# A decoder layer's up-projection: weight blocks and the T2 operand exchange their places in memory

## The chip, the cores and the metric

The kernel runs on 1 core of one Trainium2 chip. The metric is the device time of one execution in microseconds, the median of several runs. All arithmetic is in float32: each operand is split into a rounded high part and a rest (low part), and each product is three matmuls (low by high, high by low, high by high).

## The reference

One layer of a decoder trunk over 1024 tokens of width 1024: three token mixers, gated and merged, an output projection with a residual, then a convolutional feed-forward block. The change lies where the output projection ends and the up-projection begins.

```python
merged = gates[:, :, 0] * y_attn + gates[:, :, 1] * y_conv + gates[:, :, 2] * y_cross
h = h + merged @ w_out[l]

hn = rms_norm(h, ffn_norm_w[l])
up = causal_depthwise_conv(hn @ w_up[l], ffn_conv_w[l], ffn_conv_b[l])   # width 3
a, gt = jnp.split(up, 2, axis=-1)
h = h + (jax.nn.silu(gt) * a) @ w_down[l]
```

D_FF is 2816, so `hn @ w_up` has 22 pairs of 128 value columns and 128 gate columns.

## The kernel before

**Stages and engines.** The program is a list of stages. Each stage gives one function per engine (`sync`, `tensor`, `scalar`, `gpsimd`, `vector`), and every engine runs its own list in order. Engines meet at semaphores only; the order of the work is written out by hand. SyncE issues the loads. ScalarE rounds to high parts (`nc.scalar.copy` into a float32r tile), VectorE makes low parts (source less high part). SBUF addresses are given by hand with `at(name, offset, ...)`.

**Output projection (`w_out_stage`).** It has two halves of 512 columns (j = 0 and 1), each with 8 token tiles (t) of 128 tokens; a tile is 24 matmuls into one of two PSUM banks. Its weights come through a ring of 8 slots: `stage` (raw, the first 16 KiB of the memory used), `whi` (next 16 KiB) and `wlo` (next). The weights of the second half are split at j = 0, t = 7. VectorE evicts each tile with the residual added (line 2047). In the second half ScalarE stores each finished row tile to memory and squares it (lines 2011 and 326), GpSimd makes the row scale from pairs of tiles (lines 332 and 335), VectorE scales the pair (line 341, called from `scale`), and TensorE transposes it: batches 0 and 1 between the matmuls of tiles 4 and 5, batch 2 in tile 7 (line 1662), batch 3 in the next stage (`h_last_pe`, line 1685). The transposed pairs of tiles are the four buffers `xt`. Tiles 4 and 5 start with a wait for the row scaling of their batch.

**Up-projection (`up_stage`).** Each pair U of column blocks is one level of a Strassen-like scheme: seven products instead of eight, each of 12 matmuls (4 k-tiles by 3). The weight blocks 1, 2 and 4 are read from `u_raw`; 5, 6, 7 and 3 are sums and differences of blocks (`up_dve_sum`, lines 1821 to 1829, into `u_sums`). All seven are split into `u_hi` (ScalarE, line 1801) and `u_lo` (VectorE, line 1805). The moving operands are quarters of the normalised, transposed h (`act_hi`, `act_lo`) for products 1, 2 and 3 and the combinations T1 (product 5), T2 (6), T3 (7) and T4 (4). Each T has two halves q = 0, 1, and for each half a sum on VectorE (line 1747), a high part on ScalarE (line 1754) and a low part on VectorE (line 1759). `T_HALVES` gives the order of these splits, `T_SUMS` that of the sums. The T are made once, at the entry of the stage, and serve all pairs.

The accumulators of products 1, 6, 5 and 3 of a pair share one PSUM bank. After each of the first three ScalarE copies it out (s1, q1, q2: lines 1838, 1845, 1852), and the next product waits for that copy: 5 waits for `q1_done`, 3 waits for `q2_done`. In `pair_act`, the steady order of ScalarE, q1 is followed by the high parts 6 and 7 of the next pair and then by q2.

TensorE enters the stage with products 1 and 2 of pair 0. Then comes product 1 of pair 1 "ahead" (its blocks lie apart, in `u_next`), the transposes of batch 3, product 2 of pair 1 ahead, and products 6, 7, 5, 3, 4 of pair 0. From pair 1 on the order `middle` repeats: 6, 7, 5, the next pair's 1, 3, 4, the next pair's 2.

**Memory around the change.** T2 lies in the stage ring's raw slots, T3 in `whi`, T4 in `wlo`. The blocks lie in the region behind `h_rows` (`U_W`): two `u_raw` buffers, `u_hi`, `u_lo`, and then 8 KiB that `u_sums` and `u_next` share. The blocks and sums of pair 0 are made in the first half of the output projection (`first_pairs`, steps 2 to 7), the ahead parts of pair 1 at steps 8 and 9. The sums of pair 1 are made in `pair_dve` of pair 0 and wait until both ahead products are through.

**Down-projection.** Its first two pieces are split inside the last pair (`first_split`, `down_lows`); `d_stage`, `d_hi`, `d_lo` and `gs` lie in the low 28 KiB.

## Time and profile before

| | us |
|---|---|
| runs of the kernel before | 1985.51, 1983.98, 1985.40 |
| median | 1985.4 |
| profiled execution | 1986.32 |
| its span, first to last instruction | 1984.5 |

| engine | busy share of the span |
|---|---|
| TensorE matmul (PE) | 98% |
| TensorE weight load (PEld) | 83% |
| VectorE (DVE) | 55% |
| ScalarE (ACT) | 37% |
| GpSimd (POOL) | 5% |

How to read it: times of an instruction are counted from the start of the span. A busy share is a mean over stages with different limits, so it doesn't tell where an engine stood still; the views of the waits and the timeline do. A timeline row gives start, duration, engine, line of the kernel, operation, output and inputs with their shapes, and how many in a row were merged (x4). Brackets at its end hold the idle time before it and what ended it. Matmuls overlap: one lasts 0.39 us and the next starts 0.23 us after it at the full clock. The second half of the output projection starts near 1243, the up-projection at 1293, and the down-projection near 1740.

### The profile page before, as it was taken

The page shows a single profiled execution, that of the slowest core. Times are in us where ns is not written, and L with a number is a line of the kernel's source. Part 1 is how long each engine was busy: PE and PEld are TensorE (multiplying, and loading weights), DVE is VectorE, ACT ScalarE, POOL GpSimd, SP SyncE. Part 2 cuts the span into 40 slices and gives each one's busy share as a digit, 9 for nine tenths or more (in the row PEclk, how much of TensorE's full clock was granted, in tenths as well). Part 3 has the DMA queues.
Part 4 walks back from the last instruction along what each step waited for, and adds up shares of the span by engine and source line. Part 5 has one row for each costly group of instructions (what it writes and reads, how often), then busy time and mean ns, then how long its engine had stood idle before and what let it go on. Part 6 is the DMA issues. An engine that isn't in the chain of part 4 may idle for free. (4 is left out here: it accounts for less than half of the span.)

```text
span 1984.5 us, 24170 instructions
## 1 busy us (share of the span) xinstructions
PE 1939.7 (98%) x9113; PEld 1652.3 (83%) x9113; DVE 1098.7 (55%) x1413; ACT 738.3 (37%) x1324; POOL 99.1 (5%) x153
## 2 busy tenths in 40 slices
PE   6999999999999999999999999989999999999999
PEld 5788999999998887887887887768888888778887
DVE  5535532443351876896415535477878787743433
ACT  6323532432252155223523332454545454432222
POOL 1101110111010010000000010000000000000000
PEclk9999999999999998999999999989999999999999
DMA  6211221021113101102113404202222222264312
GB/s 243 96 43 43 71 70 43 12 80 48 43 65 107 43 1 43 43 22 64 43 43 101 135 22 170 96 11 96 77 82 84 74 90 69 72 245 149 111 48 74
DMA packets 112412, 152.33 MB, mean 77 GB/s; under 512 B 13705, under 2 KB 60809, under 8 KB 112329
## 3 DMA queue, kind: packets, MB, share of 16 engines
q1 hardware_dynamic: 104265, 140.60, 21.4%
q10 hardware_dynamic: 8064, 10.59, 1.4%
q8 instruction: 56, 0.92, 0.2%
q14 instruction: 27, 0.22, 0.0%
HBM read 122.73 MB, written 28.43 MB: 76 GB/s over the span
## 5 line engine op out<-in xcount | busy, mean ns | idle before, releaser
L241 PE MATMUL psum<-whi,act_lo 128*128 128x512 f32 x768 | 314.7, 410 | 3.0 <-DVE act_lo L1432 2.4
L243 PE MATMUL psum<-whi,act_hi 128*128 128x512 f32 x768 | 304.9, 397 | 0.0
L242 PE MATMUL psum<-wlo,act_hi 128*128 128x512 f32 x768 | 304.2, 396 | 0.0
L241 PEld LDWEIGHTS psum<-whi,act_lo 128*128 128x128 f32 x768 | 195.1, 254 | 18.2 <-issue 4.0
L243 PEld LDWEIGHTS psum<-whi,act_hi 128*128 128x128 f32 x768 | 195.1, 254 | 15.4
L242 PEld LDWEIGHTS psum<-wlo,act_hi 128*128 128x128 f32 x768 | 195.6, 255 | 13.0
L241 PE MATMUL psum<-act_hi,wlo 128*128 128x512 f32 x512 | 203.7, 398 | 0.0
L243 PE MATMUL psum<-act_hi,whi 128*128 128x512 f32 x512 | 200.6, 392 | 0.0
L242 PE MATMUL psum<-act_lo,whi 128*128 128x512 f32 x512 | 200.4, 391 | 0.0
L194 ACT CAST whi<-stage 128x512 fp32r<-128x512 f32 x200 | 120.1, 621 | 183.6 <-PE psum L243 175.6
L199 DVE TENSOR_TENSOR wlo<-stage,whi 128x512 fp32r<-128x512 f32 x200 | 129.0, 685 | 95.1 <-ACT whi L194 94.2
L241 PE MATMUL psum<-d_hi,gs_lo 128*128 128x512 f32 x352 | 137.3, 390 | 1.9 <-DVE d_lo L2102 1.2
L241 PE MATMUL psum<-act_hi,u_lo 128*128 128x512 f32 x344 | 136.3, 396 | 2.3 <-issue 1.5
L243 PE MATMUL psum<-d_hi,gs_hi 128*128 128x512 f32 x352 | 137.0, 389 | 0.0
L242 PE MATMUL psum<-d_lo,gs_hi 128*128 128x512 f32 x352 | 136.9, 389 | 0.0
L242 PE MATMUL psum<-act_lo,u_hi 128*128 128x512 f32 x344 | 135.9, 395 | 0.0
L243 PE MATMUL psum<-act_hi,u_hi 128*128 128x512 f32 x344 | 135.9, 395 | 0.0
L2099 DVE TENSOR_TENSOR gs_lo<-gated,gs_hi 128x1024 fp32r<-128x1024 f32 x44 | 53.9, 1225 | 145.1 <-ACT gs_hi L2085 141.7
L243 PEld LDWEIGHTS psum<-act_hi,whi 128*128 128x128 f32 x512 | 96.8, 189 | 20.8
L242 PEld LDWEIGHTS psum<-act_lo,whi 128*128 128x128 f32 x512 | 97.1, 190 | 19.1
L241 PEld LDWEIGHTS psum<-act_hi,wlo 128*128 128x128 f32 x512 | 97.1, 190 | 19.1
L241 PE MATMUL psum<-t_hi,u_lo 128*128 128x512 f32 x264 | 105.6, 400 | 7.0 <-DVE t_lo L1759 7.0
(248 smaller groups left out, 3591.1 us busy)
## 6 DMA issues: line engine op xcount, KB each, us to landing
stage<-in_w_in SPq DMA_DIRECT2D x144, 256.0 KB, 4.1
u_raw<-in_w_up SPq DMA_DIRECT2D x44, 512.0 KB, 4.6
gated_scratch<-g_buf SPq DMA_DIRECT2D x22, 512.0 KB, 2.6
gated<-gated_scratch SPq DMA_DIRECT2D x22, 512.0 KB, 3.4
d_stage<-in_w_down SPq DMA_DIRECT2D x44, 256.0 KB, 2.9
group_out<-ob ACTq DMA_DIRECT2D x24, 256.0 KB, 2.1
grp<-group_out SPq DMA_DIRECT2D x24, 256.0 KB, 3.1
stage<-in_w_mem_kv SPq DMA_DIRECT2D x16, 256.0 KB, 7.9
```

Source lines behind the costliest of these rows:

```text
L194: nc.scalar.copy(whi[:, pos, :], stage[:, pos, :]).then_inc(w_hi, 1)
L199: nc.vector.tensor_tensor(wlo[:, pos, :], stage[:, pos, :], whi[:, pos, :].bitcast(F32), ALU.subtract).then_inc(w_lo[pos % 2], 1)
L241: nc.tensor.matmul(dst, lhs[1], rhs[0], start=first, stop=False, skip_group_check=True)
L242: nc.tensor.matmul(dst, lhs[0], rhs[1], start=False, stop=False, skip_group_check=True)
L243: return nc.tensor.matmul(dst, lhs[0], rhs[0], start=False, stop=last, skip_group_check=True)
L2099: nc.vector.tensor_tensor(gs[1][pos][:], gated[:, k, :], gs[0][pos][:].bitcast(F32), ALU.subtract).then_inc(gs_lo_done, 1)
```

## The change

1. **Places.** `u_hi` moves to the bottom of memory (the ring's raw slots), and so does the fourth block sum. T2 moves behind the blocks (`U_W + 36864`), over what were the upper half of `u_lo` and the shared 8 KiB. The other three sums get places of their own. `u_next` now lies over the even `u_raw` buffer. `d_stage` moves up, into what was `xt[0]`; `d_hi` and `gs` shift within the low part. The small statistics tiles are packed, and `FREE` is rounded to 512 bytes.
2. **Output projection.** The sums of pair 0 are made at j = 1, t = 0, its casts and low parts at t = 1 and 2, the ahead parts of pair 1 at t = 3, and the sums of pair 1 at t = 6 instead of inside pair 0.
3. **TensorE.** The transposes of batch 3 come before product 1 of pair 1 ahead, not after it.
4. **VectorE and ScalarE at the entry.** The transposed copies of batch 3 come first, and the T splits after them, in a new order (`T_LOWS` is the order of the low parts). Both sums of T4 come last.
5. **Waits.** The load of pair 2 waits for both ahead products; the wait of pair 1's sums for them goes. The ahead casts wait for all seven low parts of pair 0. VectorE waits for product 5 of the last pair before the first low parts of the down-projection.

```diff
@@ -147,7 +147,7 @@
         vecs = at("vecs", SMALL + 1024, [NVECS])
-        STATS = SMALL + 1024 + (NVECS * 4 + 63) // 64 * 64
+        STATS = SMALL + 1024 + (NVECS * 4 + 31) // 32 * 32
         sumsq = at("sumsq", STATS, [NT])
@@ -156,10 +156,9 @@
         ln_sums = at("ln_sums", STATS + 384, [6])
-        row_sumsq = at("row_sumsq", STATS + 416, [NT + MT])
-        row_meansq = at("row_meansq", STATS + 480, [NT + MT])
-        row_scale = at("row_scale", STATS + 544, [NT + MT])
-        FREE = (STATS + 544 + 64 + P - 1) // P * P
+        row_stats = at("row_stats", STATS + 416, [3, NT + MT])
+        row_sumsq, row_meansq, row_scale = (row_stats[:, i, :] for i in range(3))
+        FREE = (STATS + 536 + 511) // 512 * 512
@@ -1592,8 +1591,10 @@
         T_BYTES = HALF_K * CW * 4
-        t2, t3, t4 = ([at(f"t{n}_{part}", (2 * i + j) * T_BYTES, [HALF_K, CW], F32R)
-                       for j, part in enumerate(("hi", "lo"))] for i, n in enumerate((2, 3, 4)))
+        U_W = FREE + 32768
+        t2, t3, t4 = ([at(f"t{n}_{part}", off + j * T_BYTES, [HALF_K, CW], F32R)
+                       for j, part in enumerate(("hi", "lo"))]
+                      for n, off in ((2, U_W + 36864), (3, 2 * T_BYTES), (4, 4 * T_BYTES)))
         t1_raw = at("t1_raw", ACTS + KT * S * 4, [KT, S])
@@ -1602,13 +1603,12 @@
-        U_W = FREE + 32768
         u_raw = [at(f"u_raw{par}", U_W + par * 8192, [2, KT, P]) for par in range(2)]
-        u_hi = at("u_hi", U_W + 16384, [7, HALF_K, P], F32R)
-        u_lo = at("u_lo", U_W + 16384 + 14336, [7, HALF_K, P], F32R)
-        u_sums = at("u_sums", U_W + 45056, [4, HALF_K, P])
-        u_next = [at("u_next_hi", U_W + 45056, [2, HALF_K, P], F32R),
-                  at("u_next_lo", U_W + 45056 + 4096, [2, HALF_K, P], F32R)]
+        u_hi = at("u_hi", 0, [7, HALF_K, P], F32R)
+        u_lo = at("u_lo", U_W + 16384, [7, HALF_K, P], F32R)
+        u_sums = [at(f"u_sum{i}", off, [HALF_K, P]) for i, off in
+                  enumerate((U_W + 30720, U_W + 32768, U_W + 34816, 14336))]
+        u_next = [at("u_next_hi", U_W, [2, HALF_K, P], F32R), at("u_next_lo", U_W + 4096, [2, HALF_K, P], F32R)]
         yg = at("yg", FREE, [S])
@@ -1722,8 +1722,10 @@
-        T_SUMS = [(i, q) for q in range(2) for i in (1, 2, 3, 4)]
-        T_HALVES = [(2, 0), (3, 0), (1, 0), (4, 0), (2, 1), (3, 1), (1, 1), (4, 1)]
+        T_SUMS = [(1, 0), (2, 0), (3, 0), (1, 1), (2, 1), (3, 1), (4, 0), (4, 1)]
+        T_HALVES = [(2, 0), (3, 0), (1, 0), (2, 1), (3, 1), (1, 1), (4, 0), (4, 1)]
...
+        T_LOWS = [(2, 0), (3, 0), (2, 1), (3, 1), (1, 0), (1, 1), (4, 0), (4, 1)]
@@ -1771,6 +1773,9 @@
                 sp.wait_ge(up_lo[4], U - 1)
+            if isinstance(U, int) and U == 2:
+                for i in (1, 2):
+                    sp.wait_ge(up_p[i], 2)
             for kind in range(2):
@@ -1782,7 +1787,7 @@
         def up_source(par, i):
-            return u_sums[:, S_OF[i]] if i in S_OF else up_block(par, i)
+            return u_sums[S_OF[i]][:] if i in S_OF else up_block(par, i)
@@ -1794,7 +1799,7 @@
             if ahead:
-                for n in S_OF:
+                for n in range(1, 8):
                     act.wait_ge(up_lo[n], 1)
@@ -1815,18 +1820,15 @@
                 dve.wait_ge(raw_loaded[par], 32 * half_U + 32)
-                if isinstance(U, int) and U == 1:
-                    dve.wait_ge(up_p[1], 2)
-                    dve.wait_ge(up_p[2], 2)
-                ins = nc.vector.tensor_tensor(u_sums[:, 0], value_low, up_block(par, 4), ALU.add)
+                ins = nc.vector.tensor_tensor(u_sums[0][:], value_low, up_block(par, 4), ALU.add)
             elif s == 1:
                 dve.wait_ge(up_sum, 4 * U + 1)
-                ins = nc.vector.tensor_tensor(u_sums[:, 1], u_sums[:, 0], up_block(par, 1), ALU.subtract)
+                ins = nc.vector.tensor_tensor(u_sums[1][:], u_sums[0][:], up_block(par, 1), ALU.subtract)
             elif s == 2:
-                ins = nc.vector.tensor_tensor(u_sums[:, 2], up_block(par, 1), value_low, ALU.subtract)
+                ins = nc.vector.tensor_tensor(u_sums[2][:], up_block(par, 1), value_low, ALU.subtract)
             else:
                 dve.wait_ge(up_sum, 4 * U + 2)
-                ins = nc.vector.tensor_tensor(u_sums[:, 3], up_block(par, 2), u_sums[:, 1], ALU.subtract)
+                ins = nc.vector.tensor_tensor(u_sums[3][:], up_block(par, 2), u_sums[1][:], ALU.subtract)
             ins.then_inc(up_sum, 1)
@@ -1997,11 +1999,7 @@
             def scalar(act):
-                for i in (1, 2, 6, 7, 5, 3, 4):
-                    up_act_hi(act, 0, 0, 0, i)
                 splits_act(act, turn_o + 1)
-                for i in (1, 2):
-                    up_act_hi(act, 1, 0, 1, i, True)
                 for t in range(NT):
@@ -2010,6 +2008,12 @@
                     rows_act_squares(act, hr, [t], lambda e, t: None)
+                    if t in (1, 2):
+                        for i in ((1, 2, 6), (7, 5, 3, 4))[t - 1]:
+                            up_act_hi(act, 0, 0, 0, i)
+                    if t == 3:
+                        for i in (1, 2):
+                            up_act_hi(act, 1, 0, 1, i, True)
                     if t in (4, 5):
@@ -2024,16 +2028,17 @@
-                def first_pairs(step):
...
-                    if step in (2, 3):
-                        for s in (0, 1) if step == 2 else (2, 3):
-                            up_dve_sum(dve, 0, 0, 0, s)
-                    elif step in (4, 5, 6, 7):
-                        for i in ((1, 2), (6, 7), (5, 3), (4,))[step - 4]:
+                def first_pairs(t):
...
+                    if t in (0, 6):
+                        for n in range(4):
+                            up_dve_sum(dve, t // 6, 0, t // 6, n)
+                    if t in (1, 2):
+                        for i in ((1, 2, 6), (7, 5, 3, 4))[t - 1]:
                             up_dve_lo(dve, 0, 0, i)
-                    elif step in (NT, NT + 1):
-                        up_dve_lo(dve, 1, 1, step - NT + 1, True)
+                    if t == 3:
+                        for i in (1, 2):
+                            up_dve_lo(dve, 1, 1, i, True)
@@ -2046,7 +2051,8 @@
                                                 ALU.add).then_inc(gemm_freed, 1)
-                        first_pairs(NT * j + t)
+                        if j == 1:
+                            first_pairs(t)
                         if j == 1 and t in (4, 5):
@@ -2055,16 +2061,15 @@
                 t_dve_sum(dve, 3, 0)
-                t_dve_sum(dve, 4, 0)
...
         gated = at("gated", FREE, [NU, S])
-        d_stage = at("d_stage", 0, [2, CW])
-        d_hi = at("d_hi", 2 * slot_bytes, [2, CW], F32R)
+        d_stage = at("d_stage", FREE + 90112, [2, CW])
+        d_hi = at("d_hi", 0, [2, CW], F32R)
         d_lo = at("d_lo", 4 * slot_bytes, [2, CW], F32R)
-        gs = [[at(f"gs_{part}{pos}", (6 + 4 * i + 2 * pos) * slot_bytes, [S], F32R) for pos in range(2)]
+        gs = [[at(f"gs_{part}{pos}", (8 + 4 * i + 2 * pos) * slot_bytes, [S], F32R) for pos in range(2)]
               for i, part in enumerate(("hi", "lo"))]
@@ -2131,23 +2136,22 @@
                 up_pe_2(pe, 0, 0)
-                pe.wait_ge(row_ss, hr.tile0 + NT)
-                up_pe_1(pe, 1, 1, True)
...
                 pe.wait_ge(row_scaled, hr.tile0 + NT)
...
                     h_last_pe(pe, k)
+                pe.wait_ge(row_ss, hr.tile0 + NT)
+                up_pe_1(pe, 1, 1, True)
                 up_pe_2(pe, 1, 1, True)
-                pe.wait_ge(t_lo, T_HALVES.index((2, 1)) + 1)
+                pe.wait_ge(t_lo, T_LOWS.index((2, 1)) + 1)
                 up_pe_6(pe, 0, 0)
-                pe.wait_ge(t_lo, T_HALVES.index((3, 1)) + 1)
+                pe.wait_ge(t_lo, T_LOWS.index((3, 1)) + 1)
                 up_pe_7(pe, 0, 0)
-                pe.wait_ge(t_lo, T_HALVES.index((1, 1)) + 1)
+                pe.wait_ge(t_lo, T_LOWS.index((1, 1)) + 1)
                 up_pe_5(pe, 0, 0)
...
                 up_pe_3(pe, 0, 0)
-                pe.wait_ge(t_lo, T_HALVES.index((4, 1)) + 1)
+                pe.wait_ge(t_lo, T_LOWS.index((4, 1)) + 1)
                 up_pe_4(pe, 0, 0)
@@ -2191,13 +2195,13 @@
             def scalar(act):
-                t_act_hi(act, T_HALVES[1:4])
                 for k in (0, 1, 4, 5):
                     h_last_act(act, k)
+                t_act_hi(act, T_HALVES[1:3])
                 up_s1(act, 0, 0)
-                t_act_hi(act, T_HALVES[4:7])
+                t_act_hi(act, T_HALVES[3:6])
                 h_act_hi(act, [5])
-                t_act_hi(act, T_HALVES[7:8])
+                t_act_hi(act, T_HALVES[6:8])
                 for U in range(3):
@@ -2214,12 +2218,12 @@
                 up_c11(dve, U, par)
-                if not last:
+                if not last and not start:
                     for n in range(3):
...
                     up_dve_lo(dve, U, par, 3)
-                if not last:
+                if not last and not start:
                     up_dve_sum(dve, U + 1, half_next, np, 3)
@@ -2236,25 +2240,28 @@
                 else:
+                    dve.wait_ge(up_p[5], NU)
                     for pos in range(2):
...
             def vector(dve):
-                t_dve_lo(dve, T_HALVES[0:1])
-                h_dve_lo(dve, [4])
-                t_dve_lo(dve, T_HALVES[1:4])
                 for k in (2, 3, 6, 7):
...
                 t_dve_sum(dve, 2, 1)
-                t_dve_lo(dve, T_HALVES[4:5])
+                t_dve_lo(dve, T_HALVES[0:1])
                 t_dve_sum(dve, 3, 1)
-                t_dve_lo(dve, T_HALVES[5:7])
-                h_dve_lo(dve, [5])
+                t_dve_lo(dve, T_HALVES[1:2])
+                t_dve_lo(dve, T_HALVES[3:5])
+                t_dve_lo(dve, T_HALVES[2:3])
+                t_dve_lo(dve, T_HALVES[5:6])
+                h_dve_lo(dve, [4, 5])
+                t_dve_sum(dve, 4, 0)
                 t_dve_sum(dve, 4, 1)
-                t_dve_lo(dve, T_HALVES[7:8])
+                t_dve_lo(dve, T_HALVES[6:8])
+                dve.wait_ge(t_lo, len(T_LOWS))
                 for U in range(3):
```

## Rows read from the trace of the kernel before

**Rows 1.** The page's first section: busy us (share) and instructions of each engine.
```profile
PE 1939.7 (98%) x9113; PEld 1652.3 (83%) x9113; DVE 1098.7 (55%) x1413; ACT 738.3 (37%) x1324; POOL 99.1 (5%) x153
```

**Rows 2.** TensorE's waits, 1190 to 1330: who waited for whom, total us, times, longest.
```profile
PE psum L241 <- DVE t_lo L1759: 7.0, 1, 7.0
```

**Rows 3.** Timeline of TensorE (start us, duration us, what), entry of the up-projection.
```profile
1298.53 0.39 PE L241 MATMUL psum<-act_hi,u_next_lo 128*128 128x512 f32 x1
...
1301.32 1.91 PE L1685 MATMUL psum<-ident,h_rows 128*128 128x128 f32 x16
...
1305.62 0.40 PE L243 MATMUL psum<-act_hi,u_next_hi 128*128 128x512 f32 x1
1312.99 0.79 PE L241 MATMUL psum<-t_hi,u_lo 128*128 128x512 f32 x1 [6.97 <-DVE t_lo L1759]
...
1321.48 0.48 PE L241 MATMUL psum<-act_hi,u_lo 128*128 128x512 f32 x1
...
1326.01 0.47 PE L241 MATMUL psum<-act_hi,u_lo 128*128 128x512 f32 x1 [1.49 <-issue]
```

**Rows 4.** Timeline of ScalarE, same stretch.
```profile
1319.85 1.05 ACT L1754 CAST t_hi<-xt 128x1024 fp32r<-128x1024 f32 x1 [2.80 <-DVE xt L1747]
1320.80 0.58 ACT L1845 COPY q<-psum 128x512 f32<-128x512 f32 x1
1324.21 1.22 ACT L1801 CAST u_hi<-u_sums 128x512 fp32r<-128x512 f32 x2 [2.83 <-DVE u_sums L1824]
1325.34 0.58 ACT L1852 COPY q<-psum 128x512 f32<-128x512 f32 x1
```

**Rows 5.** Timeline of VectorE, last row scaling to the last T4 sum.
```profile
1297.08 1.42 DVE L341 TENSOR_SCALAR h_rows<-h_rows,row_scale 128x1024 f32<-128x1024 f32 x2 [0.94 <-POOL row_scale L335]
1298.41 2.35 DVE L1747 TENSOR_TENSOR xt<-xt 128x1024 f32<-128x1024 f32 x2
...
1306.36 1.65 DVE L1680 TENSOR_SCALAR xt<-psum,vecs 128x256 f32<-128x256 f32 x4
1308.12 1.23 DVE L1747 TENSOR_TENSOR t_raw<-xt,xt 128x1024 f32<-128x1024 f32 x1
...
1318.60 1.21 DVE L1747 TENSOR_TENSOR xt<-xt 128x1024 f32<-128x1024 f32 x1
```

**Rows 6.** Table of stretches: length, busy us of each engine, PEclk, DMA share, GB/s.
```profile
895.50:899.00 3.50, 3.50 (x10) 2.71 (x9) 3.50 (x7) 0.00 (x0) 0.00 (x0) 0.51 0.76 214
...
1201.00:1204.00 3.00, 1.17 (x4) 0.75 (x5) 2.62 (x3) 0.88 (x1) 0.00 (x0) 1.00 0.99 362
...
1314.00:1316.00 2.00, 2.00 (x6) 1.60 (x5) 0.89 (x2) 1.90 (x2) 0.00 (x0) 0.50 0.00 0
...
1324.00:1326.00 2.00, 0.52 (x3) 0.10 (x2) 2.00 (x5) 1.79 (x4) 0.00 (x0) 1.00 0.00 0
```

**Rows 7.** Timeline of VectorE, output projection: block low parts, eviction of tile 2, scaling.
```profile
1232.57 1.28 DVE L1805 TENSOR_TENSOR u_lo<-u_sums,u_hi 128x512 fp32r<-128x512 f32 x2
...
1259.17 0.69 DVE L2047 TENSOR_TENSOR h_rows<-psum,h_rows 128x512 f32<-128x512 f32 x1 [4.15 <-PE psum L243]
1259.77 1.41 DVE L341 TENSOR_SCALAR h_rows<-h_rows,row_scale 128x1024 f32<-128x1024 f32 x2
```

**Rows 8.** Timeline of ScalarE, output projection: three block casts; read-out of a square.
```profile
1222.41 1.66 ACT L1801 CAST u_hi<-u_sums 128x512 fp32r<-128x512 f32 x3 [4.09 <-DVE u_sums L1826]
...
1261.23 0.18 ACT L326 ACTIVATION_READ_ACCUMULATOR psum<-h_rows 128x1 f32 x1
```

**Rows 9.** Timeline of TensorE: first matmul of token tile 4, second half.
```profile
1264.41 0.39 PE L241 MATMUL psum<-whi,act_lo 128*128 128x512 f32 x1
```

**Rows 10.** Timeline of TensorE, last pair: product 3 behind product 5.
```profile
1733.26 0.50 PE L241 MATMUL psum<-act_hi,u_lo 128*128 128x512 f32 x1 [0.68 <-ACT q L1852]
```

**Rows 11.** The page's DMA issues: KB each, median us to landing.
```profile
u_raw<-in_w_up SPq DMA_DIRECT2D x44, 512.0 KB, 4.6
```

**Rows 12.** Timeline of TensorE near 895: a stop in the third mixer's gate stage.
```profile
895.15 0.47 PE L241 MATMUL psum<-bact_hi,wlo 128*128 128x512 f32 x1 [1.93 <-DVE wlo L199]
```

## The prediction

> **What bounds the kernel now.** I read the page's busy shares first: TensorE is busy for 98% of the span [rows 1]. So a change pays only where TensorE stands still, or where it has to run matmuls at the low clock and nothing else would have held it up anyway. Next I read the waits of TensorE in the stretch that the diff touches, from the last product of the gate stage to the first steady pair of the up-projection. The longest by far is 7.0 us, for a low part of a T operand [rows 2]. The timeline of TensorE shows where it lies [rows 3]: the two products that run ahead for pair 1 stop at 1305.62, and product 6 of pair 0 starts at 1312.99. Two more stops follow: product 5 starts at 1321.48, and product 3 at 1326.01, after 1.49 us of idle time labelled "issue".
>
> These labels must be read against the program. Product 5 waits for q1_done, ScalarE's copy of product 6. ScalarE is in order, and that copy stands behind all T high parts: the last one starts at 1319.85, the q copy at 1320.80 [rows 4], and TensorE starts 0.1 us after the copy ends. The T high part in turn waits for the T4 difference of VectorE, which starts at 1318.60 and takes 1.21 [rows 5]. So it is VectorE's list of T work that sets 1321.48. The matmuls of products 6 and 7 ran at the low clock (0.50 in 1314 to 1316, 6 matmuls in 2 us, [rows 6]), and that cost nothing: at the high clock product 7 would only have waited longer. The 1.49 us before product 3 is the second q copy: it starts at 1325.34 because two casts for pair 1, started at 1324.21, stand ahead of it; these waited for block sums that VectorE made late [rows 4].
>
> **The change part by part.** I add up the shift of one event, the start of product 3 of pair 0 (1326.01 now). After it TensorE runs without a stop in both orders, so the span moves by that shift.
>
> First, the blocks of pair 0 now lie low in memory, in the stage buffer, which is in use until the last output-projection weights are split. So their 4 sums, 7 high casts and 7 low parts, all done beside the first half of the output projection now, move into the second half. In the first half nothing waits for what is taken away. In the second half VectorE has room, except at tile 2. There the order is: eviction of tile 2 at 1259.17 [rows 7], square on ScalarE with its read-out starting at 1261.23 [rows 8], then four casts. Three casts take 1.66, so one takes 0.62 and the next follows 0.52 later [rows 8]. The first cast ends at 1261.33 + 0.62 = 1261.95, the first low part starts at 1262.0, and four low parts, 0.60 apart (1.28 for two [rows 7]), let the row scaling of batch 0 start at 1264.4. It takes 1.41 [rows 7] and ends at 1265.8. TensorE wants it before the first matmul of tile 4, which starts at 1264.41 [rows 9]. So here is a **new stop of about 1.5 us**, and all behind it slips by that. At tile 3 two ahead casts and low parts stand before the scaling of batch 1. The eviction starts at 1265.7, the read-out of the square 2.06 later (1261.23 - 1259.17), the first cast ends 0.72 after that, two low parts take to 1269.9, the scaling to 1271.3. Tile 5 wants it when tile 4 is through: 24 matmuls of 0.23 and 1.8 for 16 transposes [rows 3] after 1265.9, at 1273.2. Hidden, with 1.9 us to spare. The four sums of pair 1 at tile 6 (four times 0.7 us) end before the eviction of tile 7: hidden.
>
> Second, TensorE's order. The last row scaling starts at 1297.08 and takes 1.42 [rows 5], thus with the slip it ends at 1300.0. TensorE would be through with products 1 and 2 of pair 0 at 1298.53 + 1.5 = 1300.0 as well [rows 3]. The 16 transposes start at 1300.1 instead of 1301.32, in spite of the slip, because product 1 of pair 1 (2.79 us, from 1298.53 to 1301.32) now follows them.
>
> Third, VectorE's list. Now it does five low parts of 1.22 us and two sums between the last scaling and its four transposed copies, which start at 1306.36 although the transposes were there three microseconds before [rows 3, 5]. After the change only the T3 sum stands between (its pair takes 2.35, one takes 1.22, one every 1.14 [rows 5]). The transposes end at 1302.0; the copies take 1.65 together, the last two wait for the last transposes, so they end at 1302.9, against 1308.01. The sum of T1 starts at 1303.0 instead of 1308.12 [rows 5]. But what was ahead of the copies is now behind. From the start of that T1 sum to the start of the last T4 sum the diff lists 12 operations: four sums (the T1 sum itself among them), six T low parts and two h low parts. The T2 sum needs the T1 sum and follows 1.26 later (1.22 and a hand-over), the other eleven steps are 1.14 each: 1.26 + 11 x 1.14 = 13.8 us. The last T4 sum starts at 1316.8, against 1318.60. Its high part on ScalarE starts at 1318.1, the q copy 0.95 later at 1319.0, and product 5 at **1319.7 against 1321.48: 1.8 us gained**.
>
> The gain at product 6 is larger and worth nothing by itself: low part (2,1) is the sixth operation, ends at 1303.0 + 1.26 + 4 x 1.14 + 1.22 = 1310.1, and product 6 starts 2.9 us earlier. TensorE is free at 1300.1 + 1.7 + 2 x 2.79 = 1307.3, so the 7.0 us stop becomes 2.8 us. What is late next is the q copy: products 6 and 7 end at 1315.7 at the high clock, and TensorE stands for up to 4 us before product 5.
>
> Fourth, the sums of pair 1 lie ready, so ScalarE is through with the casts before product 5 ends. Then only the copy itself separates product 5 from product 3. The last pair has this very case, 5 then 3 with nothing between: 0.68 us idle [rows 10]. So 1.49 - 0.68 = **0.8 us gained**. The sum is 1.8 + 0.8 = 2.6 us, the 1.5 us slip already in it.
>
> Fifth, what costs nothing. SyncE's load of pair 2 now waits until both ahead products are done, because their blocks lie in that buffer: issued near 1307.5, landed some 5 us later (median 4.6 for such a load [rows 11]), read after product 3 of pair 0, so a cover of over 10 us; behind it in the queue stand only loads and stores due later still. VectorE's added wait for product 5 in the last pair stands after an addition that already needs the copy of product 5, so it is met on arrival; behind it are the first low parts of the down-projection. The other addresses change no instruction. If one shape did change its speed by 0.1 us in each of 22 pairs and were not hidden, that would be 2.2 us either way, and I put this into the range. The final wait for all T lows holds back only an addition that follows them anyway.
>
> The clock is the unknown of the sum. After 1.93 us of idle time at 895.15 the granted clock was 0.51 from 895.5 to 899; yet TensorE was busy for only 1.17 of the 3.0 us from 1201 and kept 1.00, and 1.49 us of idle time before 1326.01 left it at 1.00 [rows 6, 12]. So the new stop of 1.5 us probably keeps the clock, the 2.8 us one probably loses it (then products 6 and 7 take up to 3 us more, within the 4 us that they would stand anyway, cost nothing), and a stop of 4 us surely loses it. A fast matmul follows the one before at 0.23 (2.79 us for 12), a slow one at half the clock at about 0.2 more. On this the Trainium skill, "TensorE: Matmul & The Clock Gate", section "What's actually happening", says that the number of slow matmuls varies from run to run of one kernel, with the phase at which it starts; by that page the two outcomes below would alternate among runs, by the rows alone I would pick the first.
>
> **The rivals.**
> (a) The clock survives the 2.8 us stop and is lost in the 4 us one. Then products 5 and 3 start slow. Six to fourteen matmuls at 0.2 us more each cost 1.2 to 2.8 us: gain 2.6 less that, the time 1984.0 to 1985.6, say 1984.7. For it: the 1201 row. Against: the 895 row.
> (b) Slower than before: the low clock lasts over all 24 matmuls of products 5 and 3, as it held well into product 6 and 7 now [rows 6]. 24 x 0.2 = 4.7 us, so 2.1 us slower, 1987.5. It decides from 13 slow matmuls on. Against: the low clock of now came with 7.0 us of idle time, not 4.
> (c) The stop at tile 4 doesn't arise, since casts and low parts overlap better than I laid them: 1.5 us more, 1981.3. Against: each link is a row of before.
> (d) The exchange of regions itself changes the pace of the pairs: 1980.6 to 1985.0.
>
> **How the numbers follow.** The profiled execution took 1986.32, of which the span is 1984.5; the sum gives a span of 1981.9 and 1983.7 for such an execution. The median of the runs is 0.9 below the profiled one: 1985.4 - 2.6 = 1982.8. Chances: forecast 0.50, (a) 0.22, (b) 0.08, (c) 0.10, (d) 0.10. The forecast's own range is 1981.8 to 1983.9, the three runs of before being 1.5 apart. The range for 8 in 10 takes in (a) and most of (c) and (d): 1980.8 to 1986.0. A measurement of this kernel can tell 0.2%, 4.0 us, from no change. Below 1981.4 lie most of (c) and a part of (d) and of the forecast: 0.14. Above 1989.4 lies only what I have not seen: 0.05. The rest, 0.81, is the same.
>
> **What would show it.** In the profile after: a wait of TensorE of 1.3 to 1.7 us at the start of token tile 4 for the row scaling; transposes right behind product 2 of pair 0 and ahead of the ahead products; product 6 some 2.9 us earlier; product 5 some 1.8 us earlier and started by a q copy that follows the last T high part; 0.7 us of idle time before product 3. Wrong would be: product 5 started by something else, an operation of the T list waiting (it is laid without gaps), or a low granted clock after product 5's start. The prediction fails altogether if TensorE meets new stops beyond the first pair.

## The result and the profile after

| | us |
|---|---|
| changed kernel, 4 runs | 1969.00, 1973.71, 1974.81, 1972.44 |
| its median | 1973.1 |
| kernel before, 4 runs beside it | 1985.51, 1983.98, 1985.40, 1987.75 |
| its median | 1985.45 |
| ratio, 95% interval | 0.9934, 0.9915 to 0.9952 |
| profiled execution of the changed kernel, its span | 1969.0, 1967.2 |

The change makes the kernel 13 us faster by the ratio, not 2.6 as forecast. The profiled execution is the fastest of its four runs; its span is 17.3 us under that of before, which is more than the medians differ.

Three markers cut these 17.3 us into parts. The eviction of token tile 2 comes at 1255.44, 3.73 us earlier than before [rows 7]: a gain that lies ahead of all that the prediction looked at. From there to product 3 of pair 0 it takes 64.22 us, against 66.84 before [rows 3, 7]: 2.62 us, the term that was forecast. And from product 3 to the first matmul of the down-projection it takes 402.59 us, against 413.57 (1326.01 to 1739.58): 10.98 us, where none was forecast.

Timeline of TensorE in the changed kernel (start, duration, what, and in brackets the idle time before), from token tile 4 to the down-projection:

```profile
1262.11 0.50 PE L240 MATMUL psum<-whi,act_lo 128*128 128x512 f32 x1 [1.27 <-DVE h_rows L340]
...
1296.31 1.97 PE L1685 MATMUL psum<-ident,h_rows 128*128 128x128 f32 x16
...
1306.38 0.50 PE L240 MATMUL psum<-t_hi,u_lo 128*128 128x512 f32 x1 [2.61 <-DVE t_lo L1761]
...
1315.93 0.47 PE L240 MATMUL psum<-act_hi,u_lo 128*128 128x512 f32 x1 [2.21 <-DVE t_lo L1761]
...
1319.66 0.47 PE L240 MATMUL psum<-act_hi,u_lo 128*128 128x512 f32 x1 [0.72 <-issue]
...
1722.25 0.50 PE L240 MATMUL psum<-d_hi,gs_lo 128*128 128x512 f32 x1 [0.93 <-DVE d_lo L2107]
```

Its waits in that stretch (who waited for whom, total us, times, longest), 1200 to 1330:

```profile
PE psum L240 <- DVE t_lo L1761: 4.8, 2, 2.6
PE psum L240 <- DVE h_rows L340: 1.3, 1, 1.3
```

The 7.0 us for a T low part [rows 2] have become two stops of 2.61 and 2.21 us, the stop before tile 4 is new (1.27), and the one before product 3 is halved (0.72, [rows 3]). The order of the other engines answers to [rows 4, 5, 7], VectorE first, then ScalarE:

```profile
1255.44 0.69 DVE L2052 TENSOR_TENSOR h_rows<-psum,h_rows 128x512 f32<-128x512 f32 x1 [0.76 <-PE psum L242]
...
1260.65 1.41 DVE L340 TENSOR_SCALAR h_rows<-h_rows,row_stats 128x1024 f32<-128x1024 f32 x2
...
1294.84 1.42 DVE L340 TENSOR_SCALAR h_rows<-h_rows,row_stats 128x1024 f32<-128x1024 f32 x2 [0.94 <-POOL row_stats L334]
1296.17 1.22 DVE L1749 TENSOR_TENSOR xt<-xt 128x1024 f32<-128x1024 f32 x1
1297.44 1.75 DVE L1680 TENSOR_SCALAR xt<-psum,vecs 128x256 f32<-128x256 f32 x4
1299.30 1.23 DVE L1749 TENSOR_TENSOR t_raw<-xt,xt 128x1024 f32<-128x1024 f32 x1
...
1311.92 2.35 DVE L1749 TENSOR_TENSOR xt<-xt 128x1024 f32<-128x1024 f32 x2
```

```profile
1313.17 2.18 ACT L1756 CAST t_hi<-xt 128x1024 fp32r<-128x1024 f32 x2 [6.14 <-DVE xt L1749]
1315.26 0.58 ACT L1847 COPY q<-psum 128x512 f32<-128x512 f32 x1
...
1318.97 0.59 ACT L1854 COPY q<-psum 128x512 f32<-128x512 f32 x1 [2.10 <-PE psum L242]
```

The large part doesn't show in any wait. It shows in the duration of the matmuls. These are groups by line over the steady pairs (1345 to 1720): line, engine, output and inputs, shapes, count, busy us, mean ns of one. First before, then after:

```profile
L241 PE MATMUL psum<-act_hi,u_lo 128*128 128x512 f32 x306 | 120.9, 395 | 0.0
...
L243 PE MATMUL psum<-t_hi,u_hi 128*128 128x512 f32 x230 | 90.8, 395 | 0.0
```

```profile
L240 PE MATMUL psum<-act_hi,u_lo 128*128 128x512 f32 x312 | 121.5, 389 | 0.7 <-ACT q L1854 0.7
...
L242 PE MATMUL psum<-t_hi,u_hi 128*128 128x512 f32 x238 | 92.6, 389 | 0.0
```

All kinds went from 395 to 389 ns, and so did the third mixer's value products, which lie ahead of the diff's entry work and multiply tiles that the diff doesn't name. Instructions that read the high part of that operand, min/median/max ns and first and last start, before and after:

```profile
L241 PE MATMUL psum<-bact_hi,wlo x192: 392/395/628, 827.1 to 1195.5; 128*128 128x512 f32 x192
```

```profile
L240 PE MATMUL psum<-bact_hi,wlo x192: 387/389/714, 826.6 to 1191.3; 128*128 128x512 f32 x192
```

A duration is only modelled, so I took the distance between starts, all fast ones of a kind averaged. In the pairs it is 233.3 ns before and 226.7 after. From product 3 of pair 0 on there are 21 times 84 matmuls; at 6.7 ns less they make 11.8 us. Two waits give back 0.8 of it (0.32 us in pair 1, where there was none, and 0.93 instead of 0.49 before the down-projection), which leaves the 10.98 above. In the value products it is 233.3 and 226.8: 576 matmuls, 3.7 us. That is the first part; what else shifts ahead of tile 2 cancels (the value products start 0.5 us earlier, and the wait for merged low parts behind them is 2.9 us instead of 2.4). In the down-projection it is 226.7 in both kernels.

### The profile page after: what moved, and what is told of

The parts are those of the page before. It is cut to its first block and busy times, and to the rows that moved or that the text cites. A ratio compares the mean times of both kernels' runs of the same rounds, so it can differ in the third digit from the quotient of the medians.

```text
span 1967.2 us, 24175 instructions
## 1 busy us (share of the span) xinstructions
PE 1920.6 (98%) x9113; PEld 1648.7 (84%) x9113; DVE 1099.0 (56%) x1413; ACT 737.9 (38%) x1324; POOL 99.3 (5%) x153
```

## The experiments

**Theory A: remainders.** The change also lowers `FREE`, the base of the whole upper region, by 128 bytes. The base of memory is at 16512, which leaves 128 by 256 (128 by 512, as the expectations count), and the low region (ring, `act_hi`, `act_lo`) shares that remainder. `FREE` before was 117888 above it, remainder 0 by 256, and is 117760 after, remainder 128. A matmul that mixes operands with different remainders is slower. **Theory B: places.** Blocks low and T2 high is what makes the pairs faster. The first run has the addresses without the exchange, the second the exchange without the addresses:

```diff
-        STATS = SMALL + 1024 + (NVECS * 4 + 63) // 64 * 64
+        STATS = SMALL + 1024 + (NVECS * 4 + 31) // 32 * 32
...
-        FREE = (STATS + 544 + 64 + P - 1) // P * P
+        FREE = (STATS + 536 + 511) // 512 * 512
```

> The kernel before, with one part of the change alone: the statistics tiles packed and FREE, the base of the upper region, lowered by 128 bytes, so that its address has the same remainder by 512 as the low region (128 instead of 256). No block, no T and no order is moved. Theory A (remainders): the matmuls that read one operand from the upper region go from one every 0.233 us to one every 0.227; 3.7 us less in the third mixer's value products and 11.0 us less in the 22 pairs, about 1970.7. Theory B (the exchange of places sets the pace of the pairs): nothing changes, 1985.4. The entry of the up-projection keeps its stops of 7.0 and 1.5 us in both.

Measured: 1974.49 against 1985.54 for the kernel before, ratio 0.9949 (0.9935 to 0.9962). Product 3 to the down-projection takes 403.02 us, 10.55 less. Three lines of the two views above:

```profile
L240 PE MATMUL psum<-act_hi,u_lo 128*128 128x512 f32 x312 | 121.4, 389 | 0.0
...
L240 PE MATMUL psum<-t_hi,u_lo 128*128 128x512 f32 x240 | 93.4, 389 | 0.0
```

```profile
L240 PE MATMUL psum<-bact_hi,wlo x192: 387/389/628, 827.4 to 1193.4; 128*128 128x512 f32 x192
```

So 128 bytes, with no block, no T and no order moved, give most of the gain: 11 us by the medians. Theory B is out as an explanation for the pairs: all but 0.4 us of their gain is here without the exchange. The forecast of 14.7 us was too high. In this profile the value products are faster, but the output projection starts only 2.0 us earlier (1194.12 against 1196.16), and product 1 of pair 0 not at all (1292.78 against 1292.87): the gain is lost to a longer wait for merged low parts (2.9 us against 2.4) and to a low clock just behind it. Table of stretches of this run (PEclk is the third number from the right):

```profile
1202.00:1206.00 4.00, 3.81 (x10) 3.07 (x11) 0.73 (x2) 0.00 (x0) 0.00 (x0) 0.60 1.03 384
1206.00:1208.00 2.00, 2.00 (x10) 1.62 (x9) 0.00 (x0) 0.00 (x0) 0.00 (x0) 0.94 1.09 362
```

This fall near 1200 stands in nine of the twelve profiles of the experiments and in neither of the two shown first, so it comes and goes with the run. From the start of the last value matmul of this kind (bact_hi by wlo) to the eviction of tile 2 it takes 64.1 us in the four profiles with the changed kernel's addresses or all of them moved alike, and no fall; in the nine with the fall it takes 65.0 to 65.7. So it costs 0.8 to 1.6 us.

The second run is the changed kernel with the old base:

```diff
-        FREE = (STATS + 536 + 511) // 512 * 512
+        FREE = (STATS + 536 + 511) // 512 * 512 + 128
```

> The changed kernel with FREE raised by 128 bytes, back to the address that it had before; everything else of the change stays. Theory A: value products 3.7 us slower again; of the pairs' matmuls those that read u_lo or T2 from the upper region are slower, between a third and all of 11.0 us, so 1980 to 1988. Theory B: as the changed kernel, 1973.1.

Measured: 1982.66, ratio 0.9987 (0.9978 to 0.9996). Start distances (table below) are slow again except for one step in three in most products: u_hi and the quarters of h both lie low now, so the middle step of a k-tile, whose own weights and next weights are both u_hi, has all its operands at one remainder. With the old base the changed kernel is 2.9 us faster than before, and my forecast of 2.6 is met. That is partly luck. The entry gives 2.5 (64.32 us from tile 2 to product 3) as forecast, but product 3 to the down-projection takes 410.61, another 2.96 less than before, which comes with the blocks' new places and which I had not counted; tile 2, at 1260.98, is 1.8 us later than before, with a low clock near 1204 ahead of it.

Three runs ask what about the addresses counts. All memory moved up by 128 (`bottom = (nc.sbuf_base + 63) // 64 * 64 + 128`):

> The changed kernel with all its memory moved up by 128 bytes: both regions have remainder 256 by 512, the upper one of the kernel before, but they are equal. If what counts is that two operands differ in their remainder: 0.227 us for each matmul, as the changed kernel, 1973.1. If what counts is the remainder 256 itself: 0.233 everywhere, over 4000 matmuls more at 0.006 us, 1990 or more.

Measured: 1970.36, ratio 0.9932 (0.9917 to 0.9947). Product 3 to the down-projection 402.82. Equality counts, not the address. Then `FREE = (STATS + 536 + 511) // 512 * 512 + 256`:

> The changed kernel with FREE raised by 256 bytes: remainders 128 (low) and 384 (upper) by 512, but equal by 256. If equality by 256 is enough: 0.227 and 1973.1. If it takes equality by 512: 0.233 for the matmuls that read from both regions, 1980 to 1988.

Measured: 1973.57, ratio 0.9940 (0.9925 to 0.9955), 403.04 in the pairs. Equality by 256 is enough. Then the same with `+ 64`:

> The changed kernel with FREE raised by 64 bytes: remainders 128 (low) and 192 (upper) by 256. A difference of 128 was slow, one of 256 was not. If a difference of 64 counts too, the value products and those steps of the pairs that read u_lo or T2 take 0.232 to 0.235 us instead of 0.227, as with 128. If only the bit of 128 counts, all stay at 0.227.

Measured: one run, 1980.58, and 410.83 us in the pairs. There a difference of 64 costs as much as one of 128 (8.2 us against 8.0), though it spreads otherwise over the steps. In the value products it doesn't: a matmul follows the one before after 229.0 ns there, against 233.0 with + 128 and 226.8 in the changed kernel, a third of the loss, so the forecast of 232 to 235 failed for them. Smaller differences were not tried.

Two runs ask which operand. T2 and the buffer behind it moved by 128:

```diff
-                      for n, off in ((2, U_W + 36864), (3, 2 * T_BYTES), (4, 4 * T_BYTES)))
+                      for n, off in ((2, U_W + 36864 + 128), (3, 2 * T_BYTES), (4, 4 * T_BYTES)))
```

> The changed kernel with T2 alone (and the buffer behind it) moved by 128 bytes: only the moving operand of product 6 has another remainder than the weights, all weights are as in the changed kernel. If any two operands that differ cost: product 6 at 0.233 us for a matmul, the six others at 0.227; 22 x 12 x 0.0065 = 1.7 us. If only the place of the weights counts: 0.227 for product 6 too.

Measured: one run, 1975.86; product 3 to the down-projection takes 2.3 us more than in the changed kernel (forecast 1.7).

`u_lo` alone moved by 128 (the tiles behind it by 128 or 256, to make room; of those TensorE reads only T2, moved by 256):

```diff
-        u_lo = at("u_lo", U_W + 16384, [7, HALF_K, P], F32R)
+        u_lo = at("u_lo", U_W + 16384 + 128, [7, HALF_K, P], F32R)
```

> The changed kernel with u_lo alone, of all that TensorE reads, moved by 128 bytes (T2 moved by 256, which was shown to cost nothing). In each k-tile the order is u_lo, u_hi, u_hi. If a step is slow whenever its own weights, the next ones or its moving operand differ in the remainder by 256: the steps of u_lo and the ones before u_lo take 0.232 to 0.234 us, the middle one stays at 0.227, in all seven products; 22 x 7 x 8 x 0.0065 = 8 us more between product 3 of pair 0 and the down-projection. If only a moving operand that differs counts, as in the run with T2 moved: only u_lo's own step is slow, 4 us.

Measured: one run, 1981.84; product 3 to the down-projection takes 7.5 us more than in the changed kernel (forecast 8).

Mean ns from the start of a matmul to the start of the next, steady pairs, worked out from the starts in the traces. In a k-tile the steps are: 1 reads the weights u_lo, 2 u_hi, 3 u_hi again; step 3 is followed by u_lo of the next k-tile.

| run | product | step 1 | step 2 | step 3 | product 3 to down-projection, us |
|---|---|---|---|---|---|
| before | 1 | 233.2 | 233.6 | 233.2 | 413.57 |
| changed kernel | 1 | 226.4 | 226.9 | 226.7 | 402.59 |
| changed, FREE + 128 | 1 | 234.2 | 226.7 | 232.4 | 410.61 |
| | 6 | 232.3 | 234.6 | 234.8 | |
| changed, FREE + 64 | 1 | 235.9 | 228.3 | 229.1 | 410.83 |
| changed, T2 + 128 | 1 | 226.6 | 226.7 | 226.7 | 404.94 |
| | 6 | 232.5 | 232.0 | 233.3 | |
| | 7 | 227.9 | 228.2 | 227.6 | |
| changed, u_lo + 128 | 1 | 234.1 | 226.7 | 232.6 | 410.13 |
| | 6 | 234.2 | 226.7 | 232.5 | |

With T2 moved, product 6 alone is slow in all three steps (and 7 by a little, which I can't explain). With u_lo moved, step 1 and the step before u_lo's are slow in all products, the middle one is not. The durations in the groups by line say the same of the run with u_lo moved, line 240, 242 and 241 being steps 1, 3 and 2:

```profile
L240 PE MATMUL psum<-act_hi,u_lo 128*128 128x512 f32 x308 | 122.3, 397 | 0.0
L242 PE MATMUL psum<-act_hi,u_hi 128*128 128x512 f32 x308 | 122.0, 396 | 0.0
L241 PE MATMUL psum<-act_lo,u_hi 128*128 128x512 f32 x308 | 119.8, 389 | 0.0
```

For a difference of 128 nearly all cases fit one rule: a step takes 227 ns when its moving operand, its own weights and the next weights, which are loaded beside it, have the same address remainder by 256, and 232 to 235 when one differs. (The load beside it is seen in the trace of the changed kernel: the weights for the matmul of 1400.60 start to load at 1400.37, when the matmul ahead of it starts. Product 7 behind the moved T2 doesn't fit, nor does its step 2 with FREE + 128, at 228.8, and with a difference of 64 the steps spread from 228 to 236.) That a moving operand counts by itself, and a weight block by itself, is shown. Why is not.

The rest of the runs is on the entry of the up-projection. **VectorE's row scaling first at tile 2:**

```diff
+                        if j == 1 and t == 2:
+                            scale(0)
                         if j == 1:
                             first_pairs(t)
...
-                        if j == 1 and t in (2, 3, 5):
+                        if j == 1 and t in (3, 5):
```

> The changed kernel with VectorE's row scaling of batch 0 ahead of the four low parts at tile 2. Theory (the stop of 1.3 us before tile 4 comes from the scaling standing behind these low parts): the stop goes, all from product 1 of pair 0 to product 3 of pair 0 comes 1.3 us earlier. Rival (tile 4 would wait for something else, or a later wait takes it up): the stop moves and product 3 starts at the same distance from the start of the output projection.

```profile
1257.26 0.69 DVE L2052 TENSOR_TENSOR h_rows<-psum,h_rows 128x512 f32<-128x512 f32 x1 [0.76 <-PE psum L242]
1257.86 0.74 DVE L340 TENSOR_SCALAR h_rows<-h_rows,row_stats 128x1024 f32<-128x1024 f32 x1
```

```profile
1306.69 0.50 PE L240 MATMUL psum<-t_hi,u_lo 128*128 128x512 f32 x1 [2.62 <-DVE t_lo L1761]
...
1316.24 0.76 PE L240 MATMUL psum<-act_hi,u_lo 128*128 128x512 f32 x1 [3.78 <-DVE t_lo L1761]
...
1322.42 0.47 PE L240 MATMUL psum<-act_hi,u_lo 128*128 128x512 f32 x1 [0.72 <-issue]
```

Measured: 1972.08, ratio 0.9935 (0.9920 to 0.9951). The stop before tile 4 is gone: from the eviction of tile 2 to product 1 of pair 0 it takes 33.68 us, against 35.18 in the changed kernel, and to product 5 58.98 against 60.49. Then the gain is lost. The first stop kept the clock (1.00 in 1306 to 1308). TensorE then stood 3.78 us before product 5 at the high clock, and after it the clock was low: product 5 to product 3 takes 6.18 us instead of 3.73. Stretches of this run:

```profile
1306.00:1308.00 2.00, 1.31 (x6) 1.07 (x7) 2.00 (x3) 1.34 (x2) 0.00 (x0) 1.00 1.11 329
...
1316.00:1320.00 4.00, 3.76 (x9) 3.01 (x10) 2.81 (x4) 1.18 (x3) 0.00 (x0) 0.50 0.00 0
```

This is rival (a) of the prediction: the clock outlives the first stop and is lost at the second. A slow product 5 isn't bound to this run or to that order of events. The changed kernel itself, run again:

> The changed kernel once more, as a base for the others. 1973.1, and, from the two parts, the remainders (11.0 us in the run of the kernel before with FREE moved) and the entry (1.8 and 0.8 us by the prediction): 13.6 us under the kernel before, less what the lower clock takes back in some runs.

```profile
1308.90 0.50 PE L240 MATMUL psum<-t_hi,u_lo 128*128 128x512 f32 x1 [2.61 <-DVE t_lo L1761]
...
1318.46 0.47 PE L240 MATMUL psum<-act_hi,u_lo 128*128 128x512 f32 x1 [2.21 <-DVE t_lo L1761]
...
1323.74 0.47 PE L240 MATMUL psum<-act_hi,u_lo 128*128 128x512 f32 x1 [0.72 <-issue]
```

Measured: 1971.78 (1968.37 to 1975.03), ratio 0.9932 (0.9919 to 0.9946). Its profile has product 5 at the same distance from tile 2 (60.53), but product 3 is 5.28 us behind it, not 3.73. The clock fell in the first stop, was back for the second, and fell once more in product 5:

```profile
1310.00:1312.00 2.00, 2.00 (x6) 1.55 (x5) 2.00 (x2) 0.00 (x0) 0.00 (x0) 0.50 0.66 161
1316.00:1318.00 2.00, 0.25 (x2) 0.00 (x0) 2.00 (x3) 1.91 (x3) 0.00 (x0) 1.00 0.00 0
1320.00:1322.00 2.00, 2.00 (x7) 1.52 (x6) 1.06 (x2) 0.00 (x0) 0.00 (x0) 0.50 0.00 0
```

**TensorE's old order** (product 1 of pair 1 ahead, before the transposes):

```diff
                 up_pe_2(pe, 0, 0)
+                pe.wait_ge(row_ss, hr.tile0 + NT)
+                up_pe_1(pe, 1, 1, True)
                 pe.wait_ge(row_scaled, hr.tile0 + NT)
...
-                pe.wait_ge(row_ss, hr.tile0 + NT)
-                up_pe_1(pe, 1, 1, True)
                 up_pe_2(pe, 1, 1, True)
```

> The changed kernel with TensorE's old order: product 1 of pair 1 ahead before the transposes of batch 3. Theory (the transposed copies start the list of T work on VectorE, which sets product 5): the transposes, and all T work behind them, come 2.7 us later; product 5 and product 3 too, 2.7 us. Rival (TensorE's order is indifferent, VectorE is held by its sums): no change at product 5.

```profile
1297.76 1.22 DVE L1749 TENSOR_TENSOR xt<-xt 128x1024 f32<-128x1024 f32 x1
1301.56 1.75 DVE L1680 TENSOR_SCALAR xt<-psum,vecs 128x256 f32<-128x256 f32 x4 [2.59 <-PE psum L1685]
1303.42 1.23 DVE L1749 TENSOR_TENSOR t_raw<-xt,xt 128x1024 f32<-128x1024 f32 x1
```

```profile
1310.50 0.79 PE L240 MATMUL psum<-t_hi,u_lo 128*128 128x512 f32 x1 [5.36 <-DVE t_lo L1761]
...
1320.06 0.47 PE L240 MATMUL psum<-act_hi,u_lo 128*128 128x512 f32 x1 [1.51 <-DVE t_lo L1761]
...
1323.75 0.47 PE L240 MATMUL psum<-act_hi,u_lo 128*128 128x512 f32 x1 [0.72 <-issue]
```

Measured: one run, 1973.23. VectorE now waits 2.59 us for the transposes, and from the eviction of tile 2 to product 5 it takes 63.09 us, 2.60 more than in the changed kernel; to product 3 66.78, 2.56 more. The time of a single run can't tell that from the usual spread, the trace can. The theory holds.

**The sums of pair 1 back in pair 0:**

```diff
-                    if t in (0, 6):
+                    if t == 0:
...
-                if not last and not start:
+                if not last:
                     for n in range(3):
```

> The changed kernel with the block sums of pair 1 back inside pair 0. Theory (two casts that wait for these sums stand before the second q copy): product 3 starts 4.4 us after product 5 instead of 3.7. Rival (the copy is held by product 5 itself): 3.7 as in the changed kernel.

Measured: one run, 1971.72; product 3 is 5.22 us behind product 5. The time by itself proves neither. The clock was low in product 5 here as in the repeated run above (5.28), so the sums had time, and the idle time before product 3 is 0.72 in both. ScalarE's rows say more:

```profile
1320.08 1.22 ACT L1806 CAST u_hi<-u_sum 128x512 fp32r<-128x512 f32 x2 [2.96 <-DVE u_sum L1826]
1321.75 0.59 ACT L1854 COPY q<-psum 128x512 f32<-128x512 f32 x1 [0.45 <-PE psum L242]
```

The two casts again wait for the sums, as in [rows 4], where the copy follows 1.13 us behind their start. By that these casts would have let the copy start at 1321.2, 4.0 us behind product 5 (1317.22), while a product 5 at the high clock is ready for it after 3.04 (1315.93 to 1318.97 in the changed kernel). So product 3 would have come some 0.9 us late, an estimate from these rows: the theory's 4.4 us and somewhat more. The rows speak for the theory; no run shows the time.

**All three stops at once.** Besides the scaling: on ScalarE q1, the casts 6 and 7 of pair 1 and q2 ahead of the T4 high parts, on VectorE the low part (2, 1) ahead of the T3 work, and c22 ahead of c11.

```diff
                 h_act_hi(act, [5])
+                up_q1(act, 0, 0)
+                up_act_hi(act, 1, 0, 1, 6)
+                up_act_hi(act, 1, 0, 1, 7)
+                up_q2(act, 0, 0)
                 t_act_hi(act, T_HALVES[6:8])
...
                 t_dve_lo(dve, T_HALVES[0:1])
+                t_dve_lo(dve, T_HALVES[3:4])
                 t_dve_sum(dve, 3, 1)
                 t_dve_lo(dve, T_HALVES[1:2])
-                t_dve_lo(dve, T_HALVES[3:5])
+                t_dve_lo(dve, T_HALVES[4:5])
...
                 dve.wait_ge(t_lo, len(T_LOWS))
+                up_c22(dve, 0, 0)
```

> As the run before, and besides: the q copies of pair 0 on ScalarE ahead of the T4 high parts, and the low part of the second half of T2 ahead of the T3 work on VectorE. Theory (product 5 is held by the q copy that stands behind the T4 casts, product 6 by VectorE's list): product 6 starts 2.3 us earlier, product 5 right behind product 7, product 3 some 0.7 us behind product 5, product 4 waits for T4 and the c22 addition instead; pair 1 starts 5 to 6 us earlier than in the changed kernel, 1967.5. Rival (VectorE's list holds everything anyway): only the 1.3 us of the run before, 1971.8.

```profile
1305.97 0.50 PE L240 MATMUL psum<-t_hi,u_lo 128*128 128x512 f32 x1 [0.41 <-DVE t_lo L1761]
...
1309.45 0.50 PE L240 MATMUL psum<-t_hi,u_lo 128*128 128x512 f32 x1 [0.46 <-DVE t_lo L1761]
...
1312.33 0.39 PE L240 MATMUL psum<-act_hi,u_lo 128*128 128x512 f32 x1
...
1315.93 0.47 PE L240 MATMUL psum<-act_hi,u_lo 128*128 128x512 f32 x1 [0.72 <-issue]
...
1320.00 0.47 PE L240 MATMUL psum<-t_hi,u_lo 128*128 128x512 f32 x1 [1.11 <-DVE t_lo L1761]
```

Measured: 1967.79 (1966.13 to 1969.26), ratio 0.9913 (0.9899 to 0.9926), the best of all. Product 5 follows product 7 without a stop, 6.9 us earlier than in the changed kernel (53.58 us behind the eviction of tile 2), product 3 7.0 us earlier. Product 4 now waits 1.11 us for T4, and in pair 1 another q copy holds it for 1.1 us; what is left is 5 us in the trace, and 4.0 in the medians against the repeated run. The last T4 sum is only 1.4 us nearer to tile 2 than in the changed kernel (56.2 against 57.6 us), and product 5 no longer cares. So the first theory holds: product 5 was held by the place of the q copy in ScalarE's list, behind casts that wait for the end of VectorE's. What the place of the copy is worth alone no run shows, since all three stops went at once; it can't be more than the stop before product 5, 2.21 us in the changed kernel and 3.78 with the clock high.

## Why the prediction was wrong

**The entry, step by step, was right.** All times here are distances from the eviction of tile 2, so that what lies ahead drops out.

| step | forecast | measured |
|---|---|---|
| row scaling of batch 0 starts | 5.2 | 5.21 |
| slip of tile 4 | 1.5 | 1.43 |
| T1 sum starts (1303.0 - 1259.17) | 43.8 | 43.86 |
| product 6 earlier by | 2.9 | 2.88 |
| product 5 earlier by | 1.8 | 1.82 |
| last T4 sum to start of product 5 | 2.9 | 2.9 |
| idle before product 3 | 0.68 | 0.72 |
| product 3 earlier by | 2.6 | 2.62 |

Product 5 was started as forecast, by the q copy behind the last T high part (1315.26, +0.58, product at 1315.93), although the bracket of TensorE's row names a T low part; that low part had long been made.

**The step that failed** stands under "Fifth, what costs nothing": "The other addresses change no instruction." The diff that lowers `FREE` was quoted in the section on the change, and I priced it at nothing. It moved every tile of the upper region to the remainder of the low one, and took 6.7 ns off each of 1848 matmuls in the pairs and 6.5 off each of 576 in the value products. Rival (d) named a change of pace, but with two errors. It was tied to the exchange of regions, where the run without the exchange shows that no exchange is needed (with the old base the exchange gives 2.96 us, with the new one nothing is left for it). And its size, 0.1 us a pair, was taken from nothing: a pair changed by 0.56 us, 84 matmuls at 6.7 ns.

The rows of before held the evidence. In the page's costliest groups the down-projection's matmuls, of the same shape, lasted 390 ns and those of the pairs 396. My own number for a product, 2.79 us for 12 [rows 3], is 232.5 ns for each, while the output projection went at 227 (1245.14 to 1264.41, 85 steps). I used both and didn't ask why they differ. A kernel that is 98% TensorE has a price per matmul as its largest term, and I took it as fixed.

What the Trainium skill says on this, in "TensorE: Matmul & The Clock Gate", section "Step-by-step: what each phase is for", would have led me the same way: TensorE has two independent read ports, and loading the next weights doesn't take bandwidth from the running matmul. The runs here don't bear out that the load is free: with the weights of one load in three moved by 128 bytes, two of three steps went from 227 to 232.6 and 234.1 ns. The measurement decides; whether the ports or something behind them meet, no run here tells.

**The clock.** The forecast gave 0.50 to a clock that falls in the first stop and is back for product 5, and 0.22 to rival (a). There are eleven profiles with the changed entry (without the one that removes the stops). In six product 3 is 3.7 us behind product 5: the changed kernel, FREE + 64, + 128, + 256, all + 128 and the transposes late. In five it is 5.2 to 6.2 us behind. Two of these, the scaling first and u_lo, are rival (a). In the other three (T2, the sums, the repeated run) the clock fell at both stops, which no case of the prediction had. So the price, 1.5 to 2.5 us, lay in the 1.2 to 2.8 of rival (a), the chance of a slow product 5 was too low, and the entry is worth 2.6 us in one run and 1.0 in another. That, and the fall near 1200, is why the median gained less than the profiled execution. Rival (b), a kernel slower than before, didn't come up; (c) neither, the stop at tile 4 is there.

**What stays open.** The medians (12.4 and 13.3 us in two sets of runs) are 4 to 5 us short of the three parts of the profile. The repeated run shows where such a difference lies, for its profile's span is 4.4 us longer: 1.6 us between product 5 and product 3, and 0.8 between the value products and tile 2, both with a low clock; 0.8 ahead of the value products and 0.9 within them, for which I have no cause; 0.3 behind product 3. Why the clock falls near 1200 in some runs and not in others no run shows.

## What to carry to other kernels

When a diff moves the base of a memory region, even by 128 bytes and for the sake of packing, every operand behind it gets another address: compare the remainders by 256 of all pairs of operands that meet in a matmul. If the same shape of matmul goes at 227 ns in one stage and 233 in another, ask why before pricing anything else. In an in-order engine, put the short copy that releases the next product ahead of long work that is not due yet. With the other two stops that was worth 4.0 us by the medians here, more than the 2.6 that the entry had gained by its new order.

## What the hardware showed that was not expected

In these runs a float32 matmul of 512 columns is followed by the next after 227 ns if its moving operand, its weights and the weights loaded beside it are at addresses equal by 256, and after 232 to 235 ns if one of them is off by 128. Off by 64 the loss in the pairs is the same in sum (8.2 us against 8.0), in the value products a third of it. The absolute address doesn't matter (all at remainder 0 or all at 128 give 227). A stop of TensorE of 2.5 to 2.6 us before product 6 kept the high clock in two profiles (the ones with the scaling first and with u_lo moved) and lost it in eight.
